# The front of a two-block transformer kernel: token transform first, half spectrum, conditioning in fp32 on four column groups

## The chip, the cores and the metric

The kernel runs on one core of one Trainium2 chip. The metric is the device time of one execution, in microseconds (us). A core has TensorE (PE; its weight loads are listed apart as PEld), VectorE (DVE), ScalarE (ACT), GpSimd (POOL) and SyncE (SP, which here only issues DMAs). Each engine runs its own instruction stream in order and meets the others through semaphores. TensorE writes into PSUM, eight banks of 512 fp32 columns on 128 partitions.

## What is computed

Two blocks follow each other. The part that the change touches is the first layer of the first block, up to the input of its feed-forward part. It works on 256 latent tokens and 256 context tokens of width 1024:

```python
sh1, sc1, g1, sh2, sc2, g2 = jnp.split(silu(c) @ w_ada[i] + b_ada[i], 6, axis=-1)   # the same for c_ctx
h = modulate(rms_norm(x, norm_gain[i, 0]), sh1, sc1)            # y * (1 + scale) + shift

def mix(h):                                                     # fnet_mixer
    b, l, _ = h.shape
    hg = h.astype(jnp.float32).reshape(b, l, FNET_GROUPS, FNET_GROUP_DIM)      # 8 groups of 128
    y = jnp.fft.fftn(hg, axes=(1, 3), norm='ortho').real
    return y.reshape(b, l, D_MODEL).astype(h.dtype) @ w_out + b_out

x = x + g1 * mix(h)
x = x + g2 * swiglu(modulate(rms_norm(x, norm_gain[i, 1]), sh2, sc2), ffn_w_in[i], ffn_w_out[i])
```

The Fourier transform runs over the tokens (256) and over the 128 channels of each group, and only its real part is kept. w_ada[i] is 1024 x 6144 fp32. The second layer (differential attention and another feed-forward) and the second block (latent attention and neighbourhood attention) follow; the change leaves them alone.

## The kernel before

Everything is fp32. A product with a weight matrix is made of three fp32r products: the weight is rounded on ACT into a high part `wh` (L364), DVE subtracts to get the low part `wl` (L369), activations have the parts `hh` and `hl` in the same way, and `product` (L384 to L386) adds hi*hi, hi*lo and lo*hi in PSUM. Weights come as slabs of 1 MB (128 partitions x 8 k-tiles x 256 columns) into four slots of `raw`, each split as two halves of 1024 columns into four slots of `wh` and `wl`. SP loads slab g only after the split of slab g-4 (`load_slab`, L375). Every order in the kernel is written by hand, engine by engine; there is no planner.

The front runs so:

- SP fetches the parameters, then four slabs of w_ada, x, ctx and the meta tokens, 20 more slabs of w_ada (all of layer 0), four of `fnet_w_out` with two slabs of layer 1's w_ada between them, then the feed-forward weights. POOL fetches the tables and the Fourier matrices.
- Conditioning (`ada_slab`, L1734): the two condition vectors, as high and low parts 4 columns wide (`condr`), are the stationary operand, and `wh` and `wl` of a slab stream through in 16 matmuls of 256 columns. Two slabs are a pair of 512 output columns in bank 6, rows 0 to 3. DVE copies the rows (L1512), `ada_turn` (L1745) turns them into columns and adds high and low, DVE adds the bias (L1523).
- `turn_x` (L1766) transposes x and ctx into channel-by-token form; DVE and ACT copy them out of PSUM. Squares (L454) and their sums over the partitions (L551, with a matrix of ones) give the norm. DVE scales (L499) and shifts (L513) into `h32`.
- `fnet_inner` (L1796) transforms over the 128 channels of a group (cosine and sine), four fp32 matmuls of 256 columns; `fnet_outer` (L1809) transforms over the tokens with both, eight matmuls of 256. The eight groups run in eight rounds, each with one pair of conditioning slabs and a turn.
- `outproj_pe` (L384 to L386) multiplies by `fnet_w_out`, eight output tiles m of 24 matmuls with 512 columns. ACT adds the bias (L1352), DVE multiplies by g1 and adds to x (L1574), ACT squares for the next norm.
- The norm "ffn0" follows (L464 and L467 on ACT, L499, L476, L515), then the feed-forward turns, each 96 products. During them the rest of layer 1's conditioning is done on DVE from half slabs that POOL fetches (`modulation`, `ada_products`).

Of the kernel before, what the change touches and what calls it, by code (L numbers as in the profile page):

```python
# [75 lines left out]
def shape_tables():  # L76
# [4 lines left out]
    for m in range(P):  # L81
        if m % 64 < 32:
            rot[m + 32, m] = -1.0
        else:
# [6 lines left out]
    dft_g = np.concatenate([np.cos(ang_g), np.sin(ang_g)], 1)  # L91
    cos_l = (np.cos(ang_l) * norm).reshape(2, P, L).transpose(1, 0, 2).reshape(P, 2 * L)
    nsin_l = (-np.sin(ang_l) * norm).reshape(2, P, L).transpose(1, 0, 2).reshape(P, 2 * L)
# [19 lines left out]
        "mask": mask, "fold": (np.arange(P)[:, None] % 2 == np.arange(2)) & (np.arange(P)[:, None] < 4),  # L113
        "dft_g": dft_g, "cos_l": cos_l, "nsin_l": nsin_l,
# [3 lines left out]
TABLE_COLS = {"ident": P, "ones": P, "fold": 2, "half": P, "rot": P, "cos_d": L, "sin_d": L, "cos_m": L2, "sin_m": L2,  # L118
              "mask": GRID_W, "dft_g": 2 * P, "cos_l": 2 * L, "nsin_l": 2 * L}
N_KEPT = 10  # L120
ROTARY_AT = sum(list(TABLE_COLS.values())[:list(TABLE_COLS).index("cos_d")])
FIRST = 2 * P + 2
KEPT = sum(list(TABLE_COLS.values())[:N_KEPT])
FOURIER = 2 * P + 4 * L
# [12 lines left out]
def slab_starts():  # L137

    stages = [("ada0", 24), ("fnet_out", 6), ("ffn0_in", 22), ("ffn0_out", 11),
# [17 lines left out]
FNET_OUT_Q = [2 * G["fnet_out"] + m + 2 * (m >= 4) + 2 * (m >= 6) for m in range(KD)]  # L157


def build(nc, d, out):  # L160

    with ExitStack() as ctx:
# [32 lines left out]
        ada_row = ex[:, 0, 1, :]  # L195
# [3 lines left out]
        condr = sb("condr", [P, KD, 4], F32R)  # L199
# [20 lines left out]
        h32 = view(4096, 4096, "p (k n) -> p k n", k=KD)  # L220
        uv = view(8192, 2048, "p (s t c) -> p s t c", s=2, t=4)
        dft_g = view(10240, 2 * P)
        cos_l = view(10240 + 2 * P, 2 * L, "p (t n) -> p t n", t=2)
        nsin_l = view(10240 + 2 * P + 2 * L, 2 * L, "p (t n) -> p t n", t=2)
# [41 lines left out]
        s_xin = sem("x_landed")  # L266
# [5 lines left out]
        s_turn_a = sem("turned_out_act")  # L272
        s_turn_v = sem("turned_out_dve")
        s_cond = sem("cond_ready")
        s_adac = sem("ada_pair_copied")
        s_adat = sem("ada_pair_turned")
# [16 lines left out]
        s_f1v = sem("fnet_inner_out_dve")  # L293
        s_f2 = sem("fnet_outer")
# [106 lines left out]
        def mod_parts(layer, n, ctx_too):  # L401
# [9 lines left out]
            "fnet": (KD, D, mod_parts(0, 0, True), None, None),  # L411
# [19 lines left out]
        SUMS = {"fnet": [(5, 0, NT)], "ffn0": [(5, 0, NT)], "diff": [(0, 0, NT)], "ffn1": [(7, 0, L)],  # L431
# [726 lines left out]
        def _(sp):  # L1158
# [6 lines left out]
            for s in range(24):  # L1165
                if s == RAW_SLOTS:
                    for a, src in enumerate((d["x"], d["ctx"])):
                        sp.dma_start(xin[:, 2 * a:2 * a + 2, :], src[0].rearrange("(t p) n -> p t n", p=P))\
                            .then_inc(s_xin, 16)
                    sp.dma_start(h32[0:N_META, 0:2, :].rearrange("p a b -> p (a b)"), d["meta_tokens_2"])\  # L1170
                        .then_inc(s_xin, 16)
                load(G["ada0"] + s, d["w_ada"][0, :, s * 256:(s + 1) * 256], KD, 256)
            for m in range(0, KD, 2):
                load(FNET_OUT_Q[m] // 2, d["fnet_w_out"][0, :, m * P:(m + 2) * P], KD, 256)
                if m in (2, 4):
                    load(FNET_OUT_Q[m] // 2 + 1, d["w_ada"][1, :, (m - 2) * P:m * P], KD, 256)
# [65 lines left out]
        def _(pool):  # L1242
            pool.wait_ge(s_xin, 48)
# [22 lines left out]
            with pool.Fori(1, 11) as i:  # L1266
                modulation(i)
# [798 lines left out]
```

## Time and profile before

| | us |
|---|---|
| median of 3 runs | 1388.44 (1387.18 to 1390.05) |
| the profiled execution | 1391.38 |
| its span | 1388.5 |
| TensorE busy in the span | 1297.6 (93%) |
| first product of the first feed-forward block starts at | 202.88 |
| one round of the transform stage (two slabs, one inner, one outer, one turn) | 9.93 |

The span is what the profiler saw between the first and the last instruction; the time of an execution is some 2.9 us longer. Matmul durations in the timeline overlap, since the engine is pipelined: what one costs in a run of many is the distance between starts. [...]

### The profile page before, as it was taken

What the parts mean: (1) busy time and instruction counts of PE and PEld (TensorE: products, weight loads), DVE (VectorE), ACT (ScalarE), POOL (GpSimd) and SP (SyncE); (2) the same over time, 40 slices, a digit from 0 to 9 for tenths busy, and PEclk for the clock granted to TensorE, in tenths of its full rate; (3) what the DMA queues carried; (4) which work ended last, traced back from release to release, by engine and by line L of the source; (5) the groups of instructions that cost most, each with busy time, mean ns of one, the idle gap of its engine ahead of it and who ended that gap; (6) DMA issues with size and microseconds to landing.
All of it is one profiled execution on the core that took longest, in us unless ns stands there. A gap on an engine that the chain in (4) does not pass through costs nothing.

```text
span 1388.5 us, 20679 instructions
## 1 busy us (share of the span) xinstructions
PE 1297.6 (93%) x7706; PEld 1076.6 (78%) x7706; DVE 800.1 (58%) x1461; ACT 608.4 (44%) x1099; POOL 85.7 (6%) x121
## 2 busy tenths in 40 slices
PE   5899989999999999989998789999989988999788
PEld 3588768888888788757994589999979666699467
DVE  5676458777777633464726755445564353355743
ACT  5444343222221222354625754444555465366642
POOL 0000021111111000010000010000010000020400
PEclk9899999999999999999998999999999999999999
DMA  9666264555555223312321034555445233074101
GB/s 326 210 206 219 94 209 130 174 181 181 169 182 170 85 93 105 105 43 80 122 91 61 1 122 152 181 183 181 160 122 176 82 91 92 1 206 159 53 31 60
DMA packets 135159, 183.58 MB, mean 132 GB/s; under 512 B 4273, under 2 KB 119264, under 8 KB 135088
## 3 DMA queue, kind: packets, MB, share of 16 engines
q1 hardware_dynamic: 127968, 156.27, 34.7%
q0 software_dynamic: 7120, 26.36, 6.0%
q8 instruction: 45, 0.74, 0.2%
q14 instruction: 26, 0.21, 0.1%
HBM read 181.57 MB, written 1.05 MB: 132 GB/s over the span
## 4 chain that ended last, share of the span: by engine, by line
PE 84%; ACT 6%; DVE 5%; issue 2%; DMA 1%; POOL 1%; SPq 0%; ACTq 0%; DVEq 0%; POOLq 0%
PE ps L384 19%; PE ps L386 19%; PE ps L385 19%; PE ps L1734 3%; PE ps L696 2%; PE ps L697 2%; PE ps L698 2%; PE ps L736 2%; PE ps L878 2%; PE ps L865 2%; PE ps L1809 2%; DVE wl L369 2%; ACT wh L364 1%; PE ps L1843 1%; DMA raw<-in_w_ada 1%
## 5 line engine op out<-in xcount | busy, mean ns | idle before, releaser
L369 DVE TENSOR_TENSOR wl<-raw,wh 128x1024 fp32r<-128x1024 f32 (+2 forms) x294 | 356.3, 1222 | 261.6 <-ACT wh L364 259.6
L364 ACT ACTIVATE wh<-raw 128x1024 fp32r<-128x1024 f32 (+2 forms) x294 | 302.8, 1044 | 338.0 <-PE ps L386 268.3
L384 PE MATMUL ps<-hh,wh 128*128 128x256 f32 (+3 forms) x1256 | 420.2, 335 | 21.0 <-DVE hl L515 14.9
L385 PE MATMUL ps<-hl,wh 128*128 128x256 f32 (+3 forms) x1256 | 412.1, 328 | 0.0
L386 PE MATMUL ps<-hh,wl 128*128 128x256 f32 (+3 forms) x1256 | 411.3, 327 | 0.0
L384 PEld LDWEIGHTS ps<-hh,wh 128*128 128x128 f32 (+1 forms) x1256 | 239.0, 190 | 48.3 <-issue 21.2
L386 PEld LDWEIGHTS ps<-hh,wl 128*128 128x128 f32 (+1 forms) x1256 | 239.4, 191 | 21.2
L385 PEld LDWEIGHTS ps<-hl,wh 128*128 128x128 f32 (+1 forms) x1256 | 238.5, 190 | 21.1 <-issue 0.2
L384 PE MATMUL ps<-ah,wh 128*128 128x256 f32 (+3 forms) x400 | 134.2, 336 | 5.1 <-DVE al L1599 3.0
L385 PE MATMUL ps<-al,wh 128*128 128x256 f32 (+3 forms) x400 | 131.9, 330 | 0.0
L386 PE MATMUL ps<-ah,wl 128*128 128x256 f32 (+3 forms) x400 | 131.9, 330 | 0.0
L384 PEld LDWEIGHTS ps<-ah,wh 128*128 128x128 f32 (+1 forms) x400 | 74.2, 186 | 19.1 <-issue 9.3
L386 PEld LDWEIGHTS ps<-ah,wl 128*128 128x128 f32 (+1 forms) x400 | 74.3, 186 | 7.7
L385 PEld LDWEIGHTS ps<-al,wh 128*128 128x128 f32 (+1 forms) x400 | 74.5, 186 | 7.4
L1599 DVE TENSOR_TENSOR al<-big,ah 128x512 fp32r<-128x512 f32 (+1 forms) x44 | 24.4, 558 | 84.1 <-ACT ah L1374 84.1
L1374 ACT ACTIVATE ah<-big 128x512 fp32r (+3 forms) x44 | 22.8, 523 | 111.6 <-PE ps L386 111.6
L794 DVE SCALAR_TENSOR_TENSOR big<-ps,par,rstd 128x256 f32<-128x256 f32 (+2 forms) x48 | 20.7, 446 | 83.3 <-ACT rstd L774 83.3
L696 PE MATMUL ps<-wh,hh 128*128 128x256 f32 (+1 forms) x224 | 64.4, 288 | 1.6 <-DVE big L794 1.4
L697 PE MATMUL ps<-wl,hh 128*128 128x256 f32 (+1 forms) x224 | 63.5, 283 | 0.0
L698 PE MATMUL ps<-wh,hl 128*128 128x256 f32 (+1 forms) x224 | 63.4, 283 | 0.0
L1734 PE MATMUL ps<-wh,condr 128*4 128x256 f32 x208 | 54.7, 300 | 9.3 <-DVE wl L369 5.1
L1651 DVE SCALAR_TENSOR_TENSOR big<-big,cond 128x256 f32<-128x256 f32 x154 | 62.8, 479 | 0.0
(178 smaller groups left out, 1642.4 us busy)
## 6 DMA issues: line engine op xcount, KB each, us to landing
raw<-in_ffn_w_in SPq DMA_DIRECT2D x44, 1024.0 KB, 5.3
raw<-in_w_ada SPq DMA_DIRECT2D x26, 1024.0 KB, 5.4
raw<-in_ffn_w_out SPq DMA_DIRECT2D x22, 1024.0 KB, 4.9
raw<-in_w_in SPq DMA_DIRECT2D x22, 1024.0 KB, 5.4
raw<-in_diff_w_in SPq DMA_DIRECT2D x12, 1024.0 KB, 5.1
big<-in_w_ada POOLq DMA_DIRECT2D x22, 512.0 KB, 4.0
ex<-in_w_ada POOLq DMA_DIRECT2D x22, 512.0 KB, 4.3
raw<-in_w_out SPq DMA_DIRECT2D x8, 1024.0 KB, 5.0
```

Source lines behind the costliest of these rows:

```text
L364: nc.scalar.activation(split_half(wh, at), raw_half(at)[0], ACT.Copy).then_inc(rounded, 1)
L369: nc.vector.tensor_tensor(split_half(wl, at), raw_half(at)[0], split_half(wh, at).bitcast(F32), ALU.subtract).then_inc(split, 1)
L384: nc.tensor.matmul(o, w_hi, m_hi, start=first, stop=False, **kw)
L385: nc.tensor.matmul(o, w_hi, m_lo, start=False, stop=False, **kw)
L386: return nc.tensor.matmul(o, w_lo, m_hi, start=False, stop=last, **kw)
L696: nc.tensor.matmul(oo, mh[:, k, tok], cols(wh), start=first, stop=False)
L697: nc.tensor.matmul(oo, mh[:, k, tok], cols(wl), start=False, stop=False)
L698: ins = nc.tensor.matmul(oo, ml[:, k, tok], cols(wh), start=False, stop=last)
L736: nc.tensor.matmul(ps[0:m, 3 + h % 2, 0:u["w"]], T[u["red"]][0:m, 0:m], sq[0:m, h % 2, 0:u["w"]], start=True, stop=True).then_inc(s_usum, 1)
L865: ins = nc.tensor.matmul(ps[:, score_bank(a, i, c), 0:a["keys"]], w, m, start=(j == 0), stop=(j == len(pairs) - 1))
L1651: ins = nc.vector.scalar_tensor_tensor(out=a, in0=w, scalar=weight, in1=a, op0=ALU.mult, op1=ALU.add)
L1734: ins = nc.tensor.matmul(ps[0:4, 6, half * 256:(half + 1) * 256].rearrange("p (h e) -> p h e", h=2), condr[:, k, :], w[:, at % SPLIT_SLOTS ...
```

## The change

Outside of the functions below nothing is altered. What it does:

- **Transform.** The inner step is now over the tokens. It takes `xin` as it lands (tokens on partitions) as the stationary operand and a trigonometric table as the moving one. The table holds 129 cosine and 127 sine columns, half of the spectrum, and is scaled by each token's reciprocal root mean square (`trig_x`), which ACT takes from four squares with a sum along the row. The channel gain (1 + scale) times the norm gain is multiplied onto the result `ab` on DVE, and the shift is added to column 0 (`inner_scaled`). The outer step is over the 128 channels: four matmuls a group, two of which read the half spectrum backwards for the other half of the columns.
- **Conditioning.** A slab is now 512 rows x 512 columns of w_ada, 1 MB, used as it lands in fp32. Its four k-tiles go each into a partition quadrant (32 rows) of bank 6: the stationary operand is a 32-column window of `condw`, zero but for two columns, and the window's place picks the rows of a pair. One copy of 128 x 512 and one turn then serve a group of 2, 2, 2, 4 or 3 pairs; `fold` adds the quadrants. The slabs come in order of need: shift and scale of channels 0 to 511, then of the rest, g1, shift and scale of the second norm, g2 and layer 1's first four blocks. They go into ten slots: the four of `raw` and places in `xin`, `ab`, `ex` and a free one, each load waiting for the former user.
- **Output projection.** For m = 0 to 3 it runs over k outside and m inside, each k as soon as its group is transformed; m = 4 to 7 as before. Twelve slabs stand among the k-steps, eight after the tiles 4 to 6, six after the last sum of the norm.
- **Loads.** x, ctx, the meta tokens and the Fourier tables go first, on SP. POOL fetches the other tables after its first four loads of `modulation`.

```diff
-    dft_g = np.concatenate([np.cos(ang_g), np.sin(ang_g)], 1)
-    cos_l = (np.cos(ang_l) * norm).reshape(2, P, L).transpose(1, 0, 2).reshape(P, 2 * L)
-    nsin_l = (-np.sin(ang_l) * norm).reshape(2, P, L).transpose(1, 0, 2).reshape(P, 2 * L)
+    trig = np.concatenate([np.cos(ang_l)[:, 0:P + 1], np.sin(ang_l)[:, 1:P]], 1) * norm
+    trig = trig.reshape(2, P, L).transpose(1, 0, 2).reshape(P, 2 * L)
...
+ADA_GROUPS = [dict(at=0, step=8, n=2, slots=("raw0", "raw1", "raw2", "raw3")),
+              dict(at=4, step=8, n=2, slots=("free", "ex", "raw2", "raw3")),
+              dict(at=16, step=4, n=2, slots=("x0", "x1", "free", "ex")),
+              dict(at=24, step=4, n=4, slots=("x0", "x1", "free", "ab0", "ab1", "x0", "x1", "free")),
+              dict(at=40, step=4, n=3, slots=("ab0", "ab1", "x0", "x1", "free", "ab0"))]
...
+                before = [j for j in range(i) if ADA_SLABS[j]["slot"] == slab["slot"]]
+                if before:
+                    sp.wait_ge(s_adau, before[-1] + 1)
+                elif slab["slot"] in ("x0", "x1"):
+                    sp.wait_ge(s_f1, KD)
+                elif slab["slot"] in ("ab0", "ab1"):
+                    sp.wait_ge(s_f2, KD)
+                elif slab["slot"] == "free":
...
+            ada_loads(0, 4)
+            for s in range(2):
+                sp.wait_ge(s_adau, s + 1)
+                fnet_load(s)
+            ada_loads(4, 10)
+            for s in (2, 3):
+                sp.wait_ge(s_adau, 4 + s + 1)
+                fnet_load(s)
...
             ffn0(0, G["ffn0_in"])
+            ada_loads(20, N_ADA_SLABS)
...
+                if t % 2 == 0:
+                    act.wait_ge(s_xin[t // 2], 16)
+                ins = nc.scalar.activation(squares, xin[:, t, :], ACT.Square, accum_out=tok_sum[:, t:t + 1])
+                link(ins)
+            act.wait_ge(v_ch, 1)
+            link(nc.scalar.activation(tok_ln, tok_sum, ACT.Ln, bias=eps_c[:, 0:1], scale=1.0 / D))
...
+            def ada_copy(gi):
+
+                dve.wait_ge(s_adau, ADA_GROUPS[gi]["end"])
+                positive(dve, s_adat, gi)
+                nc.vector.tensor_copy(ada_row, ps[:, 6, :]).then_inc(s_adac, 1)
...
+            for s in range(2):
+                for t in range(2):
+                    ins = nc.vector.tensor_scalar(trig_x[:, s, t, :], trig[:, t, :],
+                                                  tok_rstd[:, 2 * s + t:2 * s + t + 1], None, ALU.mult)
+                ins.then_inc(s_trig, 1)
...
+            def inner_scaled(g):
+
+                dve.wait_ge(s_f1a, g // 2 + 1)
+                dve.wait_ge(s_f1v, g // 2 + 1)
+                for k in range(g, g + 2):
+                    for c in range(2):
+                        ins = nc.vector.tensor_scalar(ab[:, k, c, :], ab[:, k, c, :], gsc[:, 0, 0, k, c:c + 1], None,
+                                                      ALU.mult)
+                link(ins)
+                first = ab[:, g:g + 2, :, 0:1].rearrange("p g s n -> p g (s n)")
+                nc.vector.scalar_tensor_tensor(out=first, in0=ada[:, 0, g:g + 2, :], scalar=math.sqrt(L / P),
+                                               in1=first, op0=ALU.mult, op1=ALU.add).then_inc(s_f1s, 2)
...
+                at = 30 - 2 * slab["p"]
+                for j in range(4):
+                    ins = nc.tensor.matmul(ps[32 * j:32 * j + 32, 6, :], condw[:, 4 * slab["half"] + j, at:at + 32],
+                                           ada_slot(slab["slot"])[:, j, :], start=first, stop=last)
+                ins.then_inc(s_adau, 1)
...
+                        ins = nc.tensor.matmul(ps[:, 4 + g % 2, s * L:(s + 1) * L],
+                                               xin[:, 2 * s + t, g * P:(g + 1) * P], trig_x[:, s, t, :],
+                                               start=(t == 0), stop=(t == 1))
+                ins.then_inc(s_f1, 1)
...
+                o = ps[:, 4 + g % 2, :].rearrange("p (s n) -> p s n", s=2)
+                cos_back = bass.AP(tensor=big, offset=AB_AT + g * 512 + P - 1, ap=[[13824, P], [L, 2], [-1, P - 1]])
+                sin_back = bass.AP(tensor=big, offset=AB_AT + g * 512 + L - 1, ap=[[13824, P], [L, 2], [-1, P - 1]])
+                nc.tensor.matmul(o[:, :, 0:P + 1], dft_c, ab[:, g, :, 0:P + 1], start=True, stop=False)
+                nc.tensor.matmul(o[:, :, 1:P], dft_ns, ab[:, g, :, P + 1:L], start=False, stop=True)
+                nc.tensor.matmul(o[:, :, P + 1:L], dft_c, cos_back, start=True, stop=False)
+                nc.tensor.matmul(o[:, :, P + 1:L], dft_s, sin_back, start=False, stop=True).then_inc(s_f2, 1)
...
+            fnet_inner(0)
+            fnet_inner(1)
+            ada_slab(0)
...
+            fnet_outer(0)
+            fnet_outer(1)
+            ada_slab(4)
+            fnet_dense(0)
+            fnet_outer(2)
+            ada_slab(5)
+            fnet_dense(1)
+            fnet_outer(3)
+            ada_slab(6)
+            fnet_dense(2)
...
+            for m in range(4, KD):
+                q = FNET_OUT_Q[m]
+                pe.wait_ge(split, q + 1)
+                pe.wait_ge(s_x, X_FNET + m - 3)
...
+                for i in range(12 + 3 * (m - 4), min(15 + 3 * (m - 4), 20)):
+                    ada_slab(i)
+                norm_sum(pe, "ffn0", m - 2)
...
+            for i in range(20, N_ADA_SLABS):
+                ada_slab(i)
```

TensorE in the transform stage, before (from the round of group 6 on; between the rows left out stand 32 matmuls of two slabs in turn from `wh` and `wl`):

```order
L1734 MATMUL ps<-wh,condr 4x256
L1734 MATMUL ps<-wl,condr 4x256
...
L1796 MATMUL ps<-big 128x256 x4
L1809 MATMUL ps<-big 128x256 x8
L1745 MATMUL ps<-tab,ex 128x2 x4
```

and now, the transform over the tokens (L1877) with the first conditioning group (L1834) and its turn (L1844), up to the first outer step:

```order
L1877 MATMUL ps<-big 128x256 x8
L1834 MATMUL ps<-raw,big 32x512 x4
L1877 MATMUL ps<-big 128x256 x4
...
L1844 MATMUL ps<-tab,big 128x4 x4
L1877 MATMUL ps<-big 128x256 x8
L1893 MATMUL ps<-big 128x2x129
L1894 MATMUL ps<-big 128x2x127
L1895 MATMUL ps<-big 128x2x127
L1896 MATMUL ps<-big 128x2x127
```

All inner steps now stand ahead of the first outer one, a slab is four matmuls of 512 columns, and an outer step is four of about 256.

TensorE at the end of the front, now (L589 is the sum of the norm's last two squares, `ffn0` follows):

```order
L584 MATMUL ps<-big,tab 128x512
L1844 MATMUL ps<-tab,big 128x8 x4
L589 MATMUL ps<-sq,tab 128x512 x2
L1834 MATMUL ps<-big 32x512 x24
L423 MATMUL ps<-hh,wh 128x512
```

Before, the feed-forward product stood right behind the two sums; six slabs (24 matmuls) have moved in between.

SP's loads, before:

```order
L375 DMA raw<-in_w_ada 128x8x256 x4
L1168 DMA big<-in_x 128x2x1024
L1168 DMA big<-in_ctx 128x2x1024
L1170 DMA big<-in_meta_tokens 16x1024
L375 DMA raw<-in_w_ada 128x8x256 x20
L375 DMA raw<-in_fnet_w_out 128x8x256 x2
```

and now:

```order
L1204 DMA big<-in_x 128x2x1024
L1204 DMA big<-in_ctx 128x2x1024
L1206 DMA big<-in_meta_tokens 16x1024
L1207 DMA big<-in_fourier 128x896
L1223 DMA raw<-in_w_ada 128x4x512 x4
L414 DMA raw<-in_fnet_w_out 128x8x256 x2
L1223 DMA big<-in_w_ada 128x4x512
L1223 DMA ex<-in_w_ada 128x4x512
L1223 DMA raw<-in_w_ada 128x4x512 x2
L1223 DMA big<-in_w_ada 128x4x512 x2
```

x and ctx have moved ahead of all slabs, the Fourier tables from POOL to SP, and the output projection's first weights from behind 24 slabs to behind four.

## Rows read from the trace of the kernel before

**Rows 1.** The page: busy time of the engines; 40 slices, granted clock and GB/s

```profile
PE 1297.6 (93%) x7706; PEld 1076.6 (78%) x7706; DVE 800.1 (58%) x1461; ACT 608.4 (44%) x1099; POOL 85.7 (6%) x121
...
GB/s 326 210 206 219 94 209 130 174 181 181 169 182 170 85 93 105 105 43 80 122 91 61 1 122 152 181 183 181 160 122 176 82 91 92 1 206 159 53 31 60
```

**Rows 2.** Chain of waits, start to 45 us (start us, us, what)

```profile
1.72 3.53 DMA big<-in_b_ada
...
11.89 3.59 PE ps L1734 x16
...
23.33 16.19 DMA raw<-in_w_ada
...
42.21 1.98 PE ps L551 x4
```

**Rows 3.** The same chain, 60 to 85 us

```profile
74.97 3.77 PE ps L1734 x32
78.74 1.73 PE ps L1796 x8
80.47 3.45 PE ps L1809 x16
83.92 0.98 PE ps L1745 x8
```

**Rows 4.** The same chain, 194 to 204 us

```profile
194.01 0.23 PE ps L386
...
196.32 2.20 PE ps L551 x4
...
198.55 0.70 ACT rstd L464
...
202.88 0.76 PE ps L384
```

**Rows 5.** Windows: length, busy (instructions) of PE, PEld, DVE, ACT, POOL; clock, DMA share, GB/s

```profile
25.00:50.00 25.00, 20.53 (x128) 13.51 (x128) 16.76 (x25) 18.08 (x28) 0.40 (x1) 0.86 1.06 349
50.00:70.00 20.00, 15.87 (x64) 9.87 (x64) 14.85 (x42) 7.88 (x16) 0.00 (x0) 0.74 0.33 107
70.00:140.00 70.00, 69.96 (x451) 56.61 (x450) 48.20 (x66) 33.79 (x42) 0.00 (x0) 1.00 0.65 211
...
25.00:31.00 6.00, 4.68 (x40) 3.97 (x40) 4.20 (x9) 4.58 (x10) 0.40 (x1) 1.00 1.08 373
31.50:38.00 6.50, 5.04 (x24) 2.94 (x25) 4.18 (x7) 5.26 (x9) 0.00 (x0) 0.50 1.05 352
144.00:147.00 3.00, 3.00 (x8) 2.32 (x8) 0.49 (x3) 0.00 (x0) 0.00 (x0) 0.50 1.06 349
...
203.00:208.50 5.50, 5.50 (x13) 4.31 (x14) 5.39 (x14) 2.73 (x6) 0.00 (x0) 0.50 0.91 303
```

**Rows 6.** Groups by line and shape, 0 to 203 us (count, busy, mean ns, idle before)

```profile
L369 DVE TENSOR_TENSOR wl<-raw,wh 128x1024 fp32r<-128x1024 f32 x64 | 77.2, 1244 | 31.4 <-ACT wh L364 31.4
L364 ACT ACTIVATE wh<-raw 128x1024 fp32r<-128x1024 f32 x64 | 63.3, 1047 | 47.9 <-PE ps L1734 46.0 <-DMA raw<-in_w_ada 1.9
L1734 PE MATMUL ps<-wh,condr 128*4 128x256 f32 x208 | 54.7, 300 | 9.3 <-DVE wl L369 5.1 <-DVE ex L1512 4.2
```

**Rows 7.** Timeline of TensorE, two places (start us, us, line, stationary and moving shape, records)

```profile
736.86 1.99 PE L865 MATMUL ps<-big 64*128 64x512 f32 x8 [0.56 <-ACT big L766]
...
1297.86 1.08 PE L1040 MATMUL ps<-x_ctx,big 128*64 128x256 f32 x8
1298.87 0.65 PE L1040 MATMUL ps<-x_ctx,tab 16*64 16x256 f32 x4
1299.45 0.66 PE L1051 MATMUL ps<-tab,ex 128*128 128x128 f32 x4
```

**Rows 8.** Timeline of ACT while x and ctx are turned

```profile
24.45 0.82 ACT L1320 ACTIVATE x_ctx<-ps 128x256 f32<-128x256 f32 x2 [3.97 <-PE ps L1766]
25.69 0.82 ACT L1320 ACTIVATE x_ctx<-ps 128x256 f32<-128x256 f32 x2 [0.41 <-PE ps L1766]
```

**Rows 9.** The page's DMA issues: count, KB each, median us to landing

```profile
raw<-in_w_ada SPq DMA_DIRECT2D x26, 1024.0 KB, 5.4
```

More of the change, by code:

```diff
@@ L155 @@
 UKV_G = [G["mix"] + 5, G["mix"] + 7]
-FNET_OUT_Q = [2 * G["fnet_out"] + m + 2 * (m >= 4) + 2 * (m >= 6) for m in range(KD)]
+FNET_OUT_Q = [2 * G["fnet_out"] + m for m in range(KD)]
+ADA_GROUPS = [dict(at=0, step=8, n=2, slots=("raw0", "raw1", "raw2", "raw3")),
[3 more added lines that the diff above has]
+              dict(at=40, step=4, n=3, slots=("ab0", "ab1", "x0", "x1", "free", "ab0"))]
+ADA_SLOTS = ("raw0", "raw1", "raw2", "raw3", "free", "ex", "x0", "x1", "ab0", "ab1")
+ADA_SLABS = []
+for _g, _group in enumerate(ADA_GROUPS):
+    _group.update(first=len(ADA_SLABS), pairs_before=sum(x["n"] for x in ADA_GROUPS[:_g]))
+    for _i, _slot in enumerate(_group["slots"]):
+        ADA_SLABS.append(dict(group=_g, p=_i // 2, half=_i % 2, slot=_slot,
+                              use=sum(x["slot"] == _slot for x in ADA_SLABS)))
+    _group["end"] = len(ADA_SLABS)
+N_ADA_SLABS = len(ADA_SLABS)
 def build(nc, d, out):
@@ L1173, in _ @@
[L1173 to L1176, printed above, removed]
+            for a, src in enumerate((d["x"], d["ctx"])):
+                sp.dma_start(xin[:, 2 * a:2 * a + 2, :], src[0].rearrange("(t p) n -> p t n", p=P))\
+                    .then_inc(s_xin[a], 16)
+            sp.dma_start(meta_in[0:N_META, :], d["meta_tokens_2"]).then_inc(s_xin[2], 16)
@@ new lines, in ada_loads, with fnet_load @@
+            def ada_loads(first, end):
+                for i in range(first, end):
+                    ada_load(i)
+            def fnet_load(s):
+                load(G["fnet_out"] + s, d["fnet_w_out"][0, :, s * 256:(s + 1) * 256], KD, 256)
+            ada_loads(0, 4)
[6 more added lines that the diff above has]
+                fnet_load(s)
@@ L1348, in _ @@
+            for q in range(2):
+                round_half(act, q, q)
+            for g in range(KD):
+                act.wait_ge(s_f2, g + 1)
+                nc.scalar.activation(hh[:, g, 0:NT], ps[:, 4 + g % 2, :], ACT.Copy).then_inc(s_f2a, 1)
+                if g < AHEAD - 2:
+                    round_half(act, g + 2, g + 2)
             for m, q in enumerate(FNET_OUT_Q):
@@ L1728, in _ @@
             ins.then_inc(s_turn, 1)
-            def ada_slab(at, half, q):
-                pe.wait_ge(split, q + 2)
-                for k in range(KD):
-                    for w in (wh, wl):
-                        ins = nc.tensor.matmul(
-                            ps[0:4, 6, half * 256:(half + 1) * 256].rearrange("p (h e) -> p h e", h=2),
-                            condr[:, k, :], w[:, at % SPLIT_SLOTS:at % SPLIT_SLOTS + 2, k * P:(k + 1) * P],
-                            start=(k == 0 and w is wh), stop=(k == KD - 1 and w is wl))
-                ins.then_inc(used, 2)
@@ L1832, in _, with ada_slab @@
-            outproj_pe(pe, FNET_OUT_Q, NT, X_FNET, "ffn0", lambda k: pe.wait_ge(s_f2v, k + 1),
-                       fnet_out_between)
+            def ada_slab(i):
+                slab = ADA_SLABS[i]
+                group = ADA_GROUPS[slab["group"]]
+                first, last = i == group["first"], i == group["end"] - 1
+                if first:
+                    positive(pe, s_adac, slab["group"])
+                pe.wait_ge(s_adaw[slab["slot"]], 16 * (slab["use"] + 1))
+                at = 30 - 2 * slab["p"]
[3 more added lines that the diff above has]
+                ins.then_inc(s_adau, 1)
```

421 lines of the change are left out of this document (220 added, 201 removed).

## Prediction

> **What bounds the kernel now.** I read the page first: TensorE is busy 93% of the span, and in the forty slices only the front moves data at the highest rate, 326 GB/s in the first slice [rows 1]. Then the chain of waits, in order of time, up to the first product of the first feed-forward block. That product (L384 at 202.88 us) ends the stretch that the change rebuilds, and nothing in it starts earlier because of other work: so the question is when this one matmul starts in the changed kernel. The chain falls into four pieces. Up to 45 us it is data and its splitting: a 16.19 us wait for a conditioning slab stands in it [rows 2]. From 64 to 134 us TensorE repeats one round of 9.93 us: two conditioning slabs 3.77, four inner transform matmuls (8 records, each fp32 matmul leaves two) 1.73, eight outer ones (16 records) 3.45, the turn 0.98 [rows 3]. There TensorE is the bound at full clock while DVE is busy 48 of 70 us and ACT 34 [rows 5]. From 143.7 us come the 192 output products at 0.23 us a piece. Last, from the last two sums of squares (L551 at 196.32) the norm's chain runs bare to 202.88 [rows 4], and TensorE restarts at half clock: 13 matmuls in 5.5 us, where 0.23 each would make 3.0 [rows 4, 5].
>
> **What the change costs, part by part.** I count TensorE's work in its new order and then ask of each step whether its data, its slot or another engine is late.
>
> *Inner and outer transform.* Inner stays 8 records of 256 columns a group, 1.73 us. The outer step had 16 records of 256 columns; it now has four fp32 matmuls of 258 and 254 columns, 8 records, so I price it at the inner's 1.73 as well [rows 3]. Two of the four read their moving operand backwards. No row shows a backward read; the nearest is the forward one at 1.73, and the far end is twice the time on these two, +0.9 us a group, 7 us in all. I take nothing, since the step still moves one 4-byte element a column, and keep the 7 for the range. Saved: 8 x 1.7 = 13.8 us.
>
> *Conditioning.* Before, 26 slabs of 1 MB cost 16 records each, 1.885 us, after ACT (1.05 us) and DVE (1.24 us) had split each half [rows 3, 6]. Now each is four fp32 matmuls of 512 columns and 32 output rows into the four partition quadrants, 8 records. An untiled fp32 matmul of 512 columns takes two records of 0.43 us: two of them stand as 4 records, 1.98 us with their tail [rows 2]. One after the other, four would be 3.43 us, worse than before. Two rows speak for their running side by side: L1040 writes the two halves of the partitions in turn, and 8 records of 256 columns start 1.01 us before the next shape, against 1.73 for the 8 of L1796 [rows 3]; L865, with the contraction split in halves, has 8 records of 512 columns in 1.99 us with the tail, against 3.4 in a row. So two tiles run fully at once [rows 7]. Four are shown nowhere here. I carry the pattern on: 0.86 us, and 0.15 to 0.2 for entering and leaving the tiled form (four pairs of L1040 take 1.01 where four records of L1796 make 0.86, and its last two take 0.58 for 0.43, up to L1051 [rows 7, 3]). That is 1.05 us a slab; the bounds are 0.86 and 3.43, with 1.7 if only two ever overlap. 26 slabs: 27 us for 49. The eight turns fewer (5 for 13) save 8 x 0.98.
>
> [...]
>
> *Start.* x and ctx are now fetched ahead of all slabs. The parameters are there at 5.25 us [rows 2]; at 349 to 373 GB/s [rows 5] 1 MB takes 2.8 to 3.0 us, so ctx is there by some 10.5 and the Fourier table by 12. The turning into x_lat and x_ctx, before shared by DVE and ACT at 1.24 us for two rounds [rows 8], is DVE's alone: 16 rounds, 8 pairs of about 1.05 (estimate: 1.24 less two transposes), from 8.5 to 17. ACT's four squares of 1024 columns (about 1.1 each, as L364 [rows 6]) end at 13 and are hidden. Four table scalings on DVE (0.28 each at the pace of L513) put the first inner matmul at 17.8. There TensorE is cold: in the kernel before it ran from 11.9 to 17.6 at half clock, 16 records in 3.59 us for 1.885 [rows 2]. The same costs 2.9 us here.
>
> *Up to the second half of the output projection.* From 17.8: low clock 2.9; eight inner 13.8; four slabs 4.2; a turn 1.0: outer 0 starts at 39.7. Then eight outer 13.8, eight slabs 8.4, eight k-steps of 12 products for m = 0 to 3 (96 x 0.232 = 22.2), two turns 2.0. Two places where another engine is late: the first k-step waits for four halves to be split by DVE between its other work, 1.6 us; and outer 4 waits for conditioning group 1 to be copied, turned, made a gain and multiplied into groups 4 and 5 by DVE (0.6 + 1.0 + 0.7 + 1.3), of which 2.5 us lie bare. That makes 90.2. Here a new wait appears: all four first products end together, so half 4 can be rounded (after one bias, 0.6 + 0.95) and split (1.15) only then: 2.5 us bare with the turn taken off.
>
> *To the end.* 96 products 22.2, eight slabs 8.4, the turn 1.0, three sums of squares 2.6: 126.9. The norm's chain takes as before 4.4 us from the end of the sums (198.5 to 202.88 [rows 4]) and would let the feed-forward start at 131.4. But six slabs stand before it on TensorE. The last of them goes into the slot of the first, so it is issued at 128.2, lands some 5.4 us later by the page's median [rows 9], at about 134, and TensorE is through at 135.5. The norm is thus no longer late; the slot is.
>
> *The loads.* 32 slabs and 3 MB of inputs and tables, 36 MB in all, up to there: at 349 GB/s [rows 5] 104 us of transfer from 5 us on. Each load into a used slot waits on SP for that slab's product, and SP issues in order. Going through them, no slab before the last two comes after TensorE wants it at 2.9 us each; at 3.5 the end is 141, at 4.0 it is 145.
>
> *What leaves ACT and DVE* (56 roundings and splits of 64 [rows 6] and the first norm) was mostly hidden, and counts only in that they no longer wait.
>
> **The sum.** 202.9 - 135.5 = 67.4 us earlier. TensorE is busy across the norm now, so the half-clock restart goes: -2.5. The last turn, moved into the first feed-forward turn: +1.0. At the two bare waits of 2.5 us the clock may fall; before, a wait of about 3 us ahead of 143.7 was followed by 3.4 us at half clock, 1.7 lost [rows 5]. Twice: +3.4. Together -65.5. Behind the front nothing is altered but the order on POOL, whose first four loads of the feed-forward conditioning go ahead of the tables. The profiled execution (1391.38, span 1388.5) is 2.9 above the median; against its own time the sum gives 1325.9, and against the median 1388.4 - 65.5 = **1323 us**.
>
> **Rivals.** *Only two column groups overlap:* 1.7 us a slab; the same walk ends at 152.2, so 1340 us. For it: rows show two, never four. *The groups run one after the other:* 3.43 us a slab; the walk ends at 196, so 1383 us, barely faster. Against it: both two-tile rows. *The loads bound the front:* at the 211 GB/s of 70 to 140 us a slab takes 5.0 and the end is 160.6, so 1348; but in that stretch TensorE held the slots, and where the slots were free the rate was 349 [rows 5]. *Slower than before: the clock stays down in the new front.* From 17.8 to 127 TensorE does about 103 us of work at full clock. [...] It decides against the change once some 68 us of that work run low. For it: in the front before 25 to 50 us show 0.86 and 50 to 70 us 0.74, some 17 us at half clock, 31.5 to 38 among them with TensorE busy for 5 of 6.5. Against it: in 70 to 140 us, with 4-column slabs 38% of the work, the granted clock is 1.00 [rows 5, 3]. *The change doesn't bring its order:* TensorE's order is written by hand and has no planner, so I give that nothing of its own.
>
> **How the numbers follow.** Forecast 0.74; two groups 0.10; loads 0.06; one after the other 0.05; slower 0.05. The forecast's own range is 1307 (slabs at 0.86, no clock drops, loads at 2.6) to 1332 (backward reads at their full price). The two-group case at 1340 and part of the loads' belong in 8 of 10: 1306 to 1345. A measurement tells 0.2% apart, 2.8 us: the serial case at 1383 is still faster by 5, but I leave 0.02 for no difference. Faster 0.93, same 0.02, slower 0.05.
>
> **What would show it.** The first product of the feed-forward block at 133 to 140 us; a conditioning slab 0.9 to 1.1 us of TensorE in the timeline (1.7 or 3.4 for the rivals); outer step 1.7 us; inner 0 near 18; waits of 2 to 3 us only before outer 4, before the fifth output tile and before the last slab; the granted clock 1.00 from about 25 us on, but for one or two stretches. Wrong I would be first through the slabs' price (26 times whatever it is off), next through the clock.

## The result, and the profile after

The changed kernel takes 1329.26 us (median of 4 runs, 1327.52 to 1330.77), the kernel before beside it 1389.24 (4 runs, 1387.18 to 1394.06). The ratio is 0.9554, 95% interval 0.9528 to 0.9580: 60.0 us less, where 65.5 were forecast. The profiled execution took 1327.52, its span 1325.8, against 1388.5 before: 62.7 us less by the spans. The first product of the feed-forward block (now L423) starts at 141.46 us instead of 202.88 [rows 4], and from there to the end it is 1184.4 us instead of 1185.7. So nearly all of the gain lies in the front. The second trace of the same kernel (`e_after_again` below) has 140.12 and 1187.7, so a single trace is good to 2 or 3 us only.

First the page of the changed kernel: the span, the busy time, and the granted clock in the forty slices.

```profile
span 1325.8 us, 19734 instructions
...
PE 1244.5 (94%) x7354; PEld 1023.5 (77%) x7354; DVE 732.3 (55%) x1378; ACT 550.3 (42%) x1026; POOL 85.7 (6%) x120
...
PEclk9989999999999999999989999999999999999899
```

TensorE has 53 us less of busy time than the 1297.6 before. The busy share hardly moved, since the span went down with it.

The chain of waits, changed kernel, first part of the front (start us, us, what). L1877 is the inner transform, L1834 a conditioning slab, L1844 the turn, L1893 to L1896 the four outer matmuls (the last two read backwards), L423 to L425 the products.

```profile
17.96 1.13 DVE big L1603 x4
...
19.39 5.38 PE ps L1877 x16
24.77 1.00 PE ps L1834 x8
25.77 1.92 PE ps L1877 x8
...
36.45 0.79 PE ps L1844 x8
...
46.31 2.28 DVE wl L408 x2
...
49.60 0.44 PE ps L1893 x2
50.03 0.43 PE ps L1894 x2
50.46 0.43 PE ps L1895 x2
50.89 0.43 PE ps L1896 x2
51.32 0.99 PE ps L1834 x8
```

A slab that stood in 16 records and 1.885 us of the round before [rows 3] is 8 records and 1.0 us. The outer step that took 3.45 is 1.73, and its two backward reads (L1895, L1896) take as long as the forward ones.

The same view, the rest of the front, down to the feed-forward block:

```profile
66.47 1.15 DVE big L1621 x4
...
67.94 1.23 PE ps L1893 x2
...
92.48 0.80 PE ps L1844 x8
...
94.47 1.15 DVE wl L408
95.66 0.80 PE ps L423
...
104.30 2.71 PE ps L1834 x24
...
132.52 1.04 PE ps L1834 x8
133.58 5.97 DMA big<-in_w_ada
139.59 1.94 PE ps L1834 x8
141.53 0.73 PE ps L423
```

The three waits that the prediction named are there: for DVE before outer 4 (65.8 to 67.94), for DVE's split before the fifth output tile (93.3 to 95.66), for the last slab (its load runs from 133.58 to 139.55, and TensorE stands still for the last 1.70 us of it). Three slabs in a row take 2.71 us.

The granted clock in stretches of the changed kernel (columns: stretch, its length, then busy time and instructions of PE, PEld, DVE, ACT and POOL; the last three are the clock, the DMA share, GB/s):

```profile
19.90:23.30 3.40, 3.40 (x9) 2.69 (x8) 0.00 (x0) 0.60 (x1) 0.00 (x0) 0.50 0.57 207
23.30:67.70 44.40, 41.62 (x215) 27.56 (x213) 15.94 (x34) 7.96 (x11) 0.00 (x0) 1.00 0.71 249
67.70:71.10 3.40, 3.16 (x8) 2.54 (x9) 1.42 (x6) 0.00 (x0) 0.00 (x0) 0.50 1.05 387
71.10:95.00 23.90, 22.17 (x114) 14.92 (x112) 5.04 (x9) 5.10 (x9) 0.00 (x0) 1.00 0.66 226
95.00:101.80 6.80, 6.14 (x15) 4.79 (x16) 6.80 (x8) 5.55 (x10) 3.07 (x2) 0.50 0.05 17
101.80:139.40 37.60, 35.36 (x201) 19.82 (x199) 17.83 (x31) 13.63 (x26) 4.36 (x3) 1.00 0.92 321
139.40:142.80 3.40, 3.21 (x11) 1.36 (x12) 3.33 (x9) 1.81 (x4) 0.60 (x1) 0.50 1.10 352
```

The first half-clock stretch (granted clock 0.50) begins just behind a wait of 1.22 us ahead of inner 0, each of the others at the end of one of the three waits. They last 3.4 or 6.8 us; between them the granted clock is 1.00. Note the last column of 95.0 to 101.8: 17 GB/s. The load pipe stands empty there, which matters below.

### The profile page after: what moved, and what is told of

It is laid out like the page before. It is cut to its first block, busy times and chain, and to the rows that moved or that the text cites. A ratio compares the mean times of both kernels' runs of the same rounds, so it can differ in the third digit from the quotient of the medians.

```text
span 1325.8 us, 19734 instructions
## 1 busy us (share of the span) xinstructions
PE 1244.5 (94%) x7354; PEld 1023.5 (77%) x7354; DVE 732.3 (55%) x1378; ACT 550.3 (42%) x1026; POOL 85.7 (6%) x120
## 3 DMA queue, kind: packets, MB, share of 16 engines
HBM read 181.37 MB, written 1.05 MB: 138 GB/s over the span
## 4 chain that ended last, share of the span: by engine, by line
PE 85%; ACT 5%; DVE 5%; issue 2%; POOL 1%; DMA 1%; SPq 0%; ACTq 0%; DVEq 0%; POOLq 0%
PE ps L423 20%; PE ps L425 19%; PE ps L424 19%; PE ps L734 2%; PE ps L735 2%; PE ps L736 2%; PE ps L774 2%; PE ps L916 2%; PE ps L903 2%; PE ps L1834 2%; DVE wl L408 1%; PE ps L1974 1%; PE ps L1877 1%; PE ps L926 1%; PE ps L2144 1%
## 5 line engine op out<-in xcount | busy, mean ns | idle before, releaser
L423 PE MATMUL ps<-hh,wh 128*128 128x256 f32 (+3 forms) x1256 | 421.1, 335 | 19.0 <-DVE hl L553 10.6
L408 DVE TENSOR_TENSOR wl<-raw,wh 128x1024 fp32r<-128x1024 f32 (+2 forms) x242 | 293.7, 1216 | 250.0 <-ACT wh L403 247.9
L425 PE MATMUL ps<-hh,wl 128*128 128x256 f32 (+3 forms) x1256 | 411.0, 327 | 0.0
L403 ACT ACTIVATE wh<-raw 128x1024 fp32r<-128x1024 f32 (+2 forms) x242 | 251.9, 1043 | 308.1 <-PE ps L425 271.6
L423 PEld LDWEIGHTS ps<-hh,wh 128*128 128x128 f32 (+1 forms) x1256 | 239.0, 190 | 56.5 <-issue 25.2
L425 PEld LDWEIGHTS ps<-hh,wl 128*128 128x128 f32 (+1 forms) x1256 | 239.0, 190 | 21.1
L423 PE MATMUL ps<-ah,wh 128*128 128x256 f32 (+3 forms) x400 | 134.2, 335 | 5.2 <-DVE al L1690 3.0
L425 PE MATMUL ps<-ah,wl 128*128 128x256 f32 (+3 forms) x400 | 131.8, 330 | 0.0
L423 PEld LDWEIGHTS ps<-ah,wh 128*128 128x128 f32 (+1 forms) x400 | 74.2, 186 | 19.1 <-issue 9.3
L425 PEld LDWEIGHTS ps<-ah,wl 128*128 128x128 f32 (+1 forms) x400 | 74.3, 186 | 7.7
L1743 DVE SCALAR_TENSOR_TENSOR sq<-ex,cond,sq 128x256 f32<-128x256 f32 x154 | 62.7, 476 | 0.0
```

The source lines that it names most:

```text
L403: nc.scalar.activation(split_half(wh, at), raw_half(at)[0], ACT.Copy).then_inc(rounded, 1)
L408: nc.vector.tensor_tensor(split_half(wl, at), raw_half(at)[0], split_half(wh, at).bitcast(F32), ALU.subtract).then_inc(split, 1)
L423: nc.tensor.matmul(o, w_hi, m_hi, start=first, stop=False, **kw)
L425: return nc.tensor.matmul(o, w_lo, m_hi, start=False, stop=last, **kw)
L1743: ins = nc.vector.scalar_tensor_tensor(out=a, in0=w, scalar=weight, in1=a, op0=ALU.mult, op1=ALU.add)
```

## The experiments

All kernels are the changed kernel with one edit or a few, in three sets, each timed beside the kernel before (1389.09, 1390.03 and 1389.82 us). The changed kernel itself was timed again in the first set only, so for the later sets the ratio is the fair comparison. The runs of one kernel spread over 3 to 10 us, and two readings stand beside the median: where the feed-forward block starts in the trace, and "at full clock", the span times its mean granted clock, as the median over the runs. The second is worked out, and only good for differences: it takes the half-clock stretches out. It is coarse too: the changed kernel's first four runs give 1300.9 and its second four 1299.8, so a difference of 1 us in it says nothing.

**The changed kernel once more**, no edit, as the base of the first set.

> The changed kernel once more, as the reference of this set: 1329 us, first feed-forward product near 141.5 us, a conditioning slab 1.00 us of TensorE.

1326.71 us (1325.2 to 1329.58), ratio 0.9544 (0.9523 to 0.9564); the feed-forward block starts at 140.12; at full clock 1299.8.

### The price of a slab: four, two or one column group

```diff
-   ins = nc.tensor.matmul(ps[32 * j:32 * j + 32, 6, :], condw[:, 4 * slab["half"] + j, at:at + 32],
-                          ada_slot(slab["slot"])[:, j, :], start=first, stop=last)
+   g = j % 2                # one group: j % 1, with start for j < 1 and stop for j >= 3
+   ins = nc.tensor.matmul(ps[32 * g:32 * g + 32, 6, :], condw[:, 4 * slab["half"] + j, at:at + 32],
+                          ada_slot(slab["slot"])[:, j, :], start=first and j < 2, stop=last and j >= 2)
```

The copy and the turn take 64 (or 32) rows; the work is the same, four matmuls of 512 columns a slab.

> All four matmuls of a conditioning slab write the first 32 partitions, one after the other, and the turn folds 32 rows. My theory, that four column groups run side by side: a slab 3.43 us for 1.00, and the walk that gave 196 against 135.5 gives some 60 us more, 1385 to 1392 us, about what the kernel before takes. Rival, that a slab of 1.00 us has nothing to do with the four quadrants (a short stationary operand is cheap in itself): no change, 1329.

> The four matmuls write two quadrants in turn. Theory of side by side running: a slab 1.72 us and a little, 17 us more, 1344 to 1349. Rival, that the order of the records within a pair prevents full overlap (each matmul leaves two records): a slab between 2.2 and 3.4 us, 30 to 60 us more.

One group: 1390.74 us (1387.59 to 1394.7), ratio 1.0005 (0.9993 to 1.0016). Two groups: 1348.05 (1346.23 to 1349.3), ratio 0.9698 (0.9677 to 0.9720). Their chains, one group first, a slab between an outer and a product:

```profile
51.16 0.43 PE ps L1898 x2
51.59 3.55 PE ps L1835 x8
55.14 0.43 PE ps L423
```

and two groups, three slabs in a row:

```profile
113.14 5.27 PE ps L1835 x24
118.41 0.43 PE ps L423
```

A slab is 3.55 us in one group, 5.27 / 3 = 1.76 in two, and 2.71 / 3 = 0.90 in four. So two tiles overlap in full, as L865 had it in the kernel before (8 records of 512 columns in 1.99 us [rows 7], where the 4 of L551 take 1.98 [rows 2]), and four do too. From four groups to one the kernel gets 64.0 us longer, 2.46 a slab, about what the rows say (3.43 for eight records of 0.43, less 0.96, between 0.90 in a row and 1.00 alone); the feed-forward block starts at 200.65, 60.5 later. So the quadrants do run side by side, and here they carry the whole change: with one group all the rest of it (half of the outer step, no splitting, no norm on the path, eight turns fewer) only makes up for slabs that cost 3.43 instead of 1.885.

Of the price, 8 records of 0.43 over four groups make 0.86. What stands alone takes 1.00, and the inner step behind it 1.92 instead of 1.73: 0.14 more at the slab that stands alone and 0.2 more at what follows it. The prediction's 0.15 to 0.2 for both was an estimate from L1040 (1.01 for 0.86, and 0.58 for 0.43 at its last two [rows 7, 3]). The chain of `e_fill_both` (below) shows the same 0.2 at an outer step behind a slab, 0.63 for 0.43:

```profile
63.15 0.79 PE ps L1844 x8
63.94 0.34 PE ps L423
...
65.44 1.00 PE ps L1834 x8
66.44 0.63 PE ps L1893 x2
```

The first product behind slabs takes 0.43 instead of 0.23 as well (`e_fill`, at 95.80), but not all of that comes from the slabs: behind a turn (L1844), which uses all 128 rows and columns, it is 0.34.

Against the 3.43 us of eight records one after the other, four column groups are 3.43 / 1.00 = 3.4 times as fast alone and 3.43 / 0.90 = 3.8 times in a row.

### The outer step twice

```diff
+   for turn in range(2):
        nc.tensor.matmul(o[:, :, 0:P + 1], dft_c, ab[:, g, :, 0:P + 1], start=True, stop=False)
...
```

The four outer matmuls of each group run twice; the second time overwrites the first with the same values.

> Every outer step of the transform is done twice over, 16 records a group as in the kernel before. If TensorE's own work sets the middle of the front: 8 x 1.73 = 13.8 us more, 1343. Rival, that the loads or the waits for DVE set it there: 8 us more or less, since the wait of 3 us before outer 4 and the landing of the slabs would take it up.

1337.11 us (1334.4 to 1343.17), ratio 0.9616 (0.9592 to 0.9639): 10.4 more than the base by the medians, 12.4 by the start of the feed-forward block (152.50), 13.9 at full clock (1313.7). The chain shows each of the extra passes at 0.43 a matmul, 8 x 1.73 = 13.8 in all. So the step is on the path with most or all of its price, and not with the 8 us or less of the rival; the 1343 expected lie 6 us above the median. Two of these runs had the clock at 0.985 and 0.986 where the base had 0.979 to 0.982, which is why the median shows less. Halving the outer step gave 10 to 14 us, where 13.8 were forecast.

### Where the inputs are in the queue

```diff
-            for a, src in enumerate((d["x"], d["ctx"])):
-                sp.dma_start(xin[:, 2 * a:2 * a + 2, :], ...)      # and the meta tokens, the Fourier tables
             ada_loads(0, 4)
+            for a, src in enumerate((d["x"], d["ctx"])):
+                sp.dma_start(xin[:, 2 * a:2 * a + 2, :], ...)      # and the meta tokens, the Fourier tables
```

> x, ctx, the meta tokens and the Fourier tables are fetched behind the first four conditioning slabs, as the kernel before did. TensorE waits for x some 10.8 us longer (four slabs at 2.7), and all of it is on the path: 1340. Rival, that the waits further on (outer 4, the fifth output tile, the last slab) take up a late start: 4 to 7 us, 1334 to 1336.

1338.39 us (1331.42 to 1341.39), ratio 0.9623 (0.9589 to 0.9658); at full clock 1310.6, 10.8 above the base. Its chain:

```profile
5.00 13.95 DMA big<-in_x
...
29.38 3.69 PE ps L1877 x16
```

x lands at 18.95, and inner 0 starts at 29.38, in the base's trace at 18.60. Of these 10.8 us 9.5 arrive at the feed-forward block (149.61 against 140.12), though a wait for a load stands there. The clock explains most of the missing 1.3: behind inner 0 the base has 3.4 us at half clock (two inner steps in 5.38 us) and this trace none (3.69), while its last slab falls on such a stretch (1.93 for 1.06). So the start of the front is worth nearly its full price.

### The last slab: slot or load pipe?

By the prediction the last slab is late because its load waits for the slot of the first of the six (`ab0`). The rival: the loads themselves are one late pipe, since none was in flight from 96.1 to 105.36. SP's timeline in the changed kernel from 88 us on (a row spans several issues):

```profile
105.36 2.08 SPq L1223 DMA_DIRECT2D big<-in_w_ada  x3
107.49 5.14 SPq L414 DMA_DIRECT2D raw<-in_ffn_w_in  x2
113.87 20.08 SPq L1223 DMA_DIRECT2D big<-in_w_ada  x6
```

`e_slot` gives the last slab the slot `raw2`, free since the sixth output slab was split; it also makes SP wait for the last slab's use before the third feed-forward slab is fetched, which then starts at 140.5 instead of 133.8. `e_ffn_loads` moves the two feed-forward slabs ahead of slabs 17 to 19, so that slabs 20 to 25 follow without a gap. `e_ffn_loads_slot` does both, that wait included.

```diff
-  dict(at=40, step=4, n=3, slots=("ab0", "ab1", "x0", "x1", "free", "ab0"))]
+  dict(at=40, step=4, n=3, slots=("ab0", "ab1", "x0", "x1", "free", "raw2"))]      # slot
...
-            ada_loads(10, 20)
+            ada_loads(10, 17)                                                      # ffn_loads
```

> The last conditioning slab goes into a raw slot that is free, so its load no longer waits for slab 20 to be used. My forecast's reason for the last wait (the slot's round trip): TensorE starts the feed-forward 2 to 4 us earlier, 1325 to 1327. Rival, that the loads before it (slab 24 lands at 136.8 us, one each 2.7 us from 105 us on) are what is late: slab 25 lands at 139.5 us as before, 1329, within 0.1%.

> The first two feed-forward slabs are fetched ahead of conditioning slab 17, into the stretch of 96 to 105 us in which no load runs. Load theory: slabs 20 to 24 land up to 6 us earlier, but 25 still waits for the slot until 133.4 us and lands at 138.7 at best, so 1 us or less, 1328. If the slot alone were the cause: no change at all.

> Both. Load theory with the slot as the next limit: slab 25 lands by 135, TensorE runs the six slabs through to 137.8, and the norm's chain (131.9 + 0.6 + 4.4 = 136.9) is about even; 3.5 to 5 us less, 1324 to 1326. Rival, that the norm's chain or DVE's order was the limit already: 0 to 1 us.

| | median us | ratio (95%) | at full clock | last slab issued, landed | feed-forward |
|---|---|---|---|---|---|
| base, again | 1326.71 | 0.9544 (0.9523 to 0.9564) | 1299.8 | 133.0, 139.1 | 140.12 |
| slot | 1326.38 | 0.9548 (0.9528 to 0.9569) | 1299.8 | 124.0, 138.1 | 140.06 |
| ffn_loads | 1326.53 | 0.9542 (0.9523 to 0.9560) | 1299.7 | 133.2, 138.5 | 139.50 |
| both | 1326.94 | 0.9546 (0.9528 to 0.9563) | 1298.8 | 120.9, 130.7 | 134.96 |

The chain of `e_slot` settles the first half of the question:

```profile
123.99 14.16 DMA raw<-in_w_ada
...
138.19 1.94 PE ps L1837 x8
140.13 0.73 PE ps L423
```

Issued nine microseconds earlier, the slab lands at 138.15 all the same, behind the loads ahead of it, one every 2.7 us. So the slot alone was not the cause. Nor was the pipe alone: with the feed-forward slabs out of the way, the load still waits for its slot, until 133.2. Two causes of the same length lie over each other, and only both edits together bring the last slab before TensorE wants it. Then TensorE goes through the six slabs without a gap, and its own work sets the start at 134.96; the first operands of the norm are ready at 134.13. That is 5.2 us less in the trace, but the medians show no difference (1326.94 against 1326.71), where 3.5 to 5 us were expected. Part of the 5.2 isn't the edits': ahead of the feed-forward block the base has 13.6 us at half clock and this trace 10.2, which is 1.7 us. The two waits that went are 2.5 us (0.82 and 1.70 in the base). And over the whole span that execution is level with the base's: 1320.7 at a clock of 0.984 and 1327.8 at 0.979 are 1300 both times. Where the 2.5 us go is open.

### Filling the waits for DVE

`e_fill` puts three of the slabs between the first four and the fifth output tile, into the wait for the split. `e_fill_both` fills the other wait too: half of k-step 3 and slab 8 go between the turn of group 1 and outer 4. `e_all` has these and both load edits.

```diff
             ada_turn(2)
+            for i in range(12, 15):
+                ada_slab(i)
             for m in range(4, KD):
...
-            fnet_dense(3)
+            fnet_dense(3, range(0, 2))
             ada_turn(1)
+            fnet_dense(3, range(2, 4))
+            ada_slab(8)
             fnet_outer(4)
             fnet_outer(5)
-            ada_slab(8)
```

> Conditioning slabs 12 to 14 stand before the fifth output tile instead of behind it, in the 3.3 us in which TensorE waits for half 4 to be split; the later ones move up by three. The wait is covered: 2.7 us, and the half-clock stretch of 95.0 to 101.8 us behind it goes, 3.4 us: 1323. Rival, that the clock falls for another reason there: 2.7 us only, 1326.5.

> Besides, the turn of group 1 stands in the middle of k-step 3, and slab 8 behind it, so that DVE has the gains ready sooner and TensorE something to do before outer 4. The wait there was 2.3 us, followed by 3.4 us at half clock: 3 to 4 us less than the former, 1319 to 1320. Rival: the end of the front is set by the loads and gives none of it back, 1323.

> The two fills, the feed-forward loads ahead of slab 17 and the free slot for the last slab. If each removes what the other makes late: 1314 to 1318. Rival: they share the same slack, 1319 or more.

| | median us (range) | ratio (95%) | at full clock | feed-forward |
|---|---|---|---|---|
| fill | 1323.38 (1318.05 to 1326.2) | 0.9508 (0.9484 to 0.9532) | 1296.8 | 134.29 |
| fill_both | 1319.78 (1317.66 to 1323.49) | 0.9497 (0.9479 to 0.9516) | 1295.6 | 131.02 |
| all | 1319.10 (1314.41 to 1319.5) | 0.9473 (0.9453 to 0.9493) | 1295.4 | 130.89 |

`e_fill`, the chain at the place and the windows behind it:

```profile
92.30 0.79 PE ps L1844 x8
93.09 2.71 PE ps L1834 x24
95.80 0.43 PE ps L423
```

```profile
93.00:100.00 7.00, 7.00 (x43) 4.17 (x44) 6.77 (x10) 5.15 (x11) 1.65 (x1) 1.00 1.00 355
```

The fifth tile starts at 95.80, where it started at 95.66 in the changed kernel's first trace; but three slabs (2.7 us) are done by then, and the clock that had been at half for 6.8 us is at full. The stretch also carries 355 GB/s instead of 17, because three slots come free 11 us earlier, and with them the whole pipe of loads moves: slab 17 is issued at 94.2 instead of 105.4, and the last one at 127.9 instead of 133.0. One edit removes the wait, the clock's fall and the hole in the loads. The fall does belong to the wait: in all nine traces that have the wait of 2.39 us before the fifth tile the clock goes to half there for 3.4 or 6.8 us, in the three that fill it never; likewise for the 2.2 us before outer 4, in ten traces against none of two.

For 2.4 us of wait that is 5.8 at the start of the feed-forward block against the base, 3.3 by the medians and 3.0 at full clock. Of the 5.8, 1.7 aren't the edit's: behind outer 4, where the two kernels are alike, the base's trace has 6.8 us at half clock and this one 3.4. The second wait, filled as well, gives another 3.6 by the medians and 3.3 by the start of the feed-forward block (1.2 at full clock). By its ratio the first fill alone isn't clear of the base (0.9484 to 0.9532 against 0.9523 to 0.9564), nor are the two fills clear of each other; both together are (0.9479 to 0.9516), and the slowest run of `e_fill_both`, 1323.49, is below the fastest of the changed kernel's eight, 1325.2.

`e_all`, TensorE's timeline, at slab 17 and at the end of the front:

```profile
102.08 1.07 PE L1837 MATMUL ps<-big 128*32 128x512 f32 x8 [1.34 <-DMA big<-in_w_ada]
...
123.60 2.07 PE L589 MATMUL ps<-sq,tab 128*128 128x512 f32 x4
125.60 4.50 PE L1837 MATMUL ps<-big 128*32 128x512 f32 x40
129.91 1.04 PE L1837 MATMUL ps<-raw,big 128*32 128x512 f32 x8
130.89 0.50 PE L423 MATMUL ps<-hh,wh 128*128 128x512 f32 x1
```

Here all six slabs follow without a wait, and TensorE goes over the norm with no break. In `e_fill_both` TensorE waits for the last slab longer than in any other trace:

```profile
130.02 1.07 PE L1834 MATMUL ps<-big 128*32 128x512 f32 x8 [2.86 <-DMA big<-in_w_ada]
```

But with the load edits the two feed-forward slabs stand ahead of slab 17, which keeps TensorE waiting for 1.34 us (first row above). So 2.86 us of wait are exchanged for 1.34, and in sum no gain shows beyond `e_fill_both` (1295.4 against 1295.6 at full clock; the start in the trace, 130.89 against 131.02, holds 1.7 us more of half clock). `e_all` has the lowest median, by 0.7 us, and is the best kernel of the study: 1319.10, 7.6 us under the changed kernel's own second measurement and 10.2 under its first, 71 under the kernel before. It lies just above the 1314 to 1318 that were expected of it, two of its five runs (1314.4, 1314.5) inside. Between it and `e_fill_both` these runs can't choose; against the changed kernel it is clear (0.9453 to 0.9493 against 0.9523 to 0.9564).

## Why the prediction was right, and where it was off

The time, 1329.3, lies in the range (1306 to 1345), 6 us above the forecast 1323. The mechanism was the forecast one; the rivals fell by the experiments: four groups overlap, the loads held TensorE up only at the end of the front, the clock fell for 17 us in the front and not throughout. That the sum comes so near is in part luck: several terms below are off by 1 to 3 us and cancel.

- **Slab.** 1.05 us forecast, 0.90 in a row to 1.00 alone, and 0.2 at what follows it: within 0.15 of the step, either way.
- **Inner and outer.** 1.73 each, right, but for the 0.2 behind a slab. The backward reads are free (0.43 as forward), so the 7 us kept for them in the range weren't needed.
- **Turn.** 0.98 forecast, 0.80.
- **Start.** The first inner matmul is at 19.39, not at 17.8 (18.60 in the second trace). The step that failed is the turning of x and ctx, from 8.5 to 17 by the forecast: DVE's first copy starts at 9.36, since it waits for the first turned round, and the last ends at 18.0. The price of a pair was nearly right: the pairs follow each other every 1.2 us, some of them after 0.86 to 0.9, on average 1.09 where 1.05 was estimated. Behind the table scalings inner 0 also waits for the copy of the meta tokens (to 19.29), a wait of 0.2 us that the sum left out. `e_x_late` shows that a later start is paid nearly in full.
- **Cold start.** 2.9 us were taken from the kernel before, where L1734's records start every 0.21 us from 11.89 to 17.4 and every 0.12 behind; the half clock was read off that pace, while the window of that stretch shows a granted clock of 1.00. Here the clock is at full just ahead of inner 0 (16.4 to 19.8) and falls for 3.4 us; the first two inner steps take 5.38 us instead of 3.46, so the price was 1.9. In `e_x_late`, `e_one_group` and `e_ffn_loads_slot` it doesn't fall there at all (3.69).
- **First half.** 90.2 forecast, 91.9 with one of the clock's falls; 93.28 measured, of which 1.6 are the start; the rest cancels (-1.0 at the cold start, -0.8 at the first k-step, +0.2 behind each slab). The waits of 2.5 us before outer 4 and before the fifth tile are 2.2 and 2.4. The 1.6 us before the first k-step is not there as such: apart from the fifth tile the products wait twice for DVE's splits, 0.8 us in all.
- **Clock.** Two falls of 1.7 us were forecast. The first cost that (3.4 us at half), the second twice as much (6.8 us), and a third came at the last slab (139.4 to 142.8). That third is the restart that I had taken off the sum (-2.5) as gone: TensorE was to be busy across the norm and wasn't. It falls partly on the slab (1.94 us instead of 1.04) and so counts in the front and not behind it. That it came was chance: the second trace has the same wait of 1.70 us and no fall, and the slab takes 1.06. How long a fall lasts was chance too: in the second trace it is 6.8 us behind outer 4 and 3.4 before the fifth tile, the other way round.
- **The last slab.** Forecast issued at 128.2, with the clock's falls 131.6, and landed 5.4 later; measured 133.58 and 5.97 later. The wait was there, and the reason was half of it. I had walked the loads through for need only, at 2.9 us each, and found none late before the last two. They go at 2.71, but in the second half no slot comes free until the three slabs behind the fifth tile are used (no load is in flight from 96.1 to 105.36), so slab 24 comes 0.74 us late too, and the last one could not have landed before some 138 by any slot (`e_slot`).
- **The sum.** Start of the feed-forward block: 135.5 forecast, 138.9 with the clock's falls, 141.46 measured, +2.6. Behind it -1.5 forecast, -1.3 measured. Together -62.7 by the spans where -65.5 was forecast. The remaining 2.7 up to the medians' -60.0 is no step of the sum: the profiled execution before stood 2.1 us above its median, the one after 1.7 below its own, and the execution is 2.9 us longer than its span before and 1.7 after. The -1.3 behind the block's start is within the scatter of single traces: in the second it is +2.0. One slip stands in the walk itself: 128.2, 5.4 and a slab of 1.05 make 134.7, not 135.5.

The lower end of the range was not needed: it held the slabs at 0.86 throughout and no fall of the clock. Behind the wait for the last slab the clock is hard to forecast: it fell behind 1.70 us here (139.4) and behind 1.53 in `e_slot`, and not behind 1.70 in `e_after_again` nor behind 2.00 in `e_fill`.

## What to carry to other kernels

A product with a few stationary columns should go over all four column groups: 0.9 to 1.0 us instead of 3.4 for 4 x 512 fp32 columns. Count that price before the savings around it: with one group it ate all of them (1390.74 us against 1389.09 before). Look at a short bare wait on TensorE not for its own length alone but for what it drags along, the clock behind it and the slots that come free later: the two waits of 2.2 and 2.4 us, filled, were worth 6.9 us by the medians, and independent work that is needed anyway was all it took to fill them. Where two causes of the same length lie over each other (a slot and the queue of loads), taking away either shows nothing in the trace, so try both together before calling one harmless; and check by the medians that what the trace shows is there.

## What the runs showed of the hardware that was not expected

- A short wait of TensorE, filled, brought the clock back: behind 2.39 us before the fifth tile it went to half in nine traces of nine, behind 2.2 us before outer 4 in ten of ten, and at neither place where other work filled the wait.
- Four column groups overlap in full in fp32: 24 matmul records of 512 columns each a 0.43 us in 2.71 us where one after the other would take 10.3; two groups take 5.27.
- A moving operand that is read backwards costs nothing: 0.43 us (L1895, L1896) beside 0.43 and 0.44 forwards (L1893, L1894).
- Most of the scatter of this kernel's runs is the clock's. Over the five runs of `e_all` the mean granted clock is 0.983 in the three of 1319.1 to 1319.5 us and 0.987 in the two of 1314.4 and 1314.5; over those of the two load edits it is 0.984 at 1322.5 and 0.978 at 1329.4. Span times clock differs by 0.8 us at most among the runs of `e_all` and by 1.1 between the other two, though the times differ by 5 and 7; the runs of `e_x_late` have the widest times, 10 us, and 2.8 us of it are left. Why a run gets more or fewer of the 3.4 us stretches the traces don't tell.
